# A two-block transformer step on one core: first expert choice by single heads, zero products on TensorE, other places for early weights, state stores on SyncE

## The reference

```python
q = (xb @ w_q).reshape(P_TOKEN_BLOCK, P_HEADS, 2, P_DKEY // 2)
s = jnp.einsum('tphd,phnd->tphn', q, subkeys)
s1, i1 = lax.top_k(s[:, :, 0], P_TOPK)
s2, i2 = lax.top_k(s[:, :, 1], P_TOPK)
cand = (s1[..., :, None] + s2[..., None, :]).reshape(...)
cidx = (i1[..., :, None] * P_NKEYS + i2[..., None, :]).reshape(...)
top, pos = lax.top_k(cand, P_TOPK)
eidx = jnp.take_along_axis(cidx, pos, axis=-1)
g = jax.nn.softmax(top, axis=-1)
act = jax.nn.gelu(jnp.einsum('tped,td->tpe', u[eidx], xb))
return jnp.einsum('tpe,tped->td', g * act, v[eidx])
```

## Time and profile before

| | us |
|---|---|
| three timed runs | 2357.81, 2358.45, 2362.10 |
| median | 2358.45 |
| profiled execution | 2352.93 |
| its span, first to last instruction | 2351.0 |

### The profile page before, as it was taken

The page is one execution under the profiler, slowest core; times in us unless marked ns, Lnnn a source line. Parts: engine busy times, 40 slices in busy tenths (PEclk is TensorE's granted clock), DMA queues, the critical chain, the costliest instruction groups (busy, mean ns, idle before and its releaser), DMA issues. The chain is left out here.

```text
span 2351.0 us, 28978 instructions
## 1 busy us (share of the span) xinstructions
PE 1575.8 (67%) x9366; PEld 844.4 (36%) x9366; DVE 1567.6 (67%) x4325; ACT 841.5 (36%) x2753; POOL 858.4 (37%) x772
## 2 busy tenths in 40 slices
PE   8888976885855446656756677797766445555555
PEld 6775633653521112324522344455433102100010
DVE  2357987556768876565697567864865897665654
ACT  2324354533323223443233435533322334232232
POOL 0013343333325343333335333343544444444351
PEclk8998988998877778877878798888888777777776
DMA  9979999999999999999999999999999999999996
GB/s 388 408 262 415 380 400 405 422 421 401 412 421 421 421 422 421 421 422 405 420 419 372 418 421 421 419 421 415 395 420 422 417 422 421 421 421 421 422 422 276
DMA packets 145003, 956.47 MB, mean 407 GB/s; under 512 B 17749, under 2 KB 20437, under 8 KB 35797
## 3 DMA queue, kind: packets, MB, share of 16 engines
q0 software_dynamic: 110592, 805.36, 82.7%
q1 hardware_dynamic: 28928, 145.20, 15.3%
q10 hardware_dynamic: 5332, 4.07, 0.8%
HBM read 951.67 MB, written 2.89 MB: 406 GB/s over the span
## 5 line engine op out<-in xcount | busy, mean ns | idle before, releaser
L825 POOL DMA_INDIRECT rows<-in_uv,eidx x768 | 858.2, 1117 | 1453.7 <-PE acc L913 1075.0
L1488 DVE CUSTOM_DVE_ANT_0 rows<-rows,xrep 128x1024 f32<-128x1024 f32 x768 | 913.2, 1223 | 403.6 <-DMA rows<-in_uv,eidx 370.1
L913 PE MATMUL acc<-rows,diag 128*32 128x512 f32 x3072 | 754.5, 742 | 513.2 <-ACT diag L1167 477.6
L913 PEld LDWEIGHTS acc<-rows,diag 128*32 128x32 f32 x3072 | 154.7, 126 | 1008.6 <-ACT diag L1167 634.3
L1167 ACT ACTIVATE act_out<-act_in 128x2 f32<-128x2 f32 x384 | 77.7, 202 | 978.8 <-DVE act_in L1488 930.6
L843 PE MATMUL bank<-wt,hT 128*128 128x256 f32 x888 | 207.4, 394 | 22.2 <-DMA wt<-in_attn_w_qkv 6.9
L1167 ACT ACT_TABLE_LOAD x120 | 154.0, 1283 | 167.0 <-DVE act_in L1488 86.7
L1167 ACT ACTIVATE diag<-small,wv 128x32 f32<-128x32 f32 x768 | 204.8, 314 | 12.5
L843 PEld LDWEIGHTS bank<-wt,hT 128*128 128x128 f32 x888 | 174.0, 198 | 63.2 <-issue 25.8
L843 PE MATMUL bank<-hT,wt 128*128 128x256 f32 (+1 forms) x896 | 182.6, 369 | 15.7 <-ACT hT L1167 8.2
L1167 ACT ACTIVATE wv<-act_out,gate 128x1 f32<-128x1 f32 x768 | 184.3, 287 | 12.6
(11 more groups left out here) (186 smaller groups left out, 1375.8 us busy)
## 6 DMA issues: line engine op xcount, KB each, us to landing
wt<-in_ada_w SPq DMA_DIRECT2D x24, 1024.0 KB
wt<-in_peer_w_q SPq DMA_DIRECT2D x24, 1024.0 KB
rows<-in_ada_w SPq DMA_DIRECT2D x36, 512.0 KB, 15.0
wt<-in_mlstm_w_in SPq DMA_DIRECT2D x12, 1024.0 KB
rows<-in_uv,eidx POOLq DMA_INDIRECT x768
wt<-in_attn_w_qkv SPq DMA_DIRECT2D x12, 1024.0 KB
rows<-in_mlstm_w_in SPq DMA_DIRECT2D x21, 512.0 KB, 15.9
rows<-in_peer_w_q SPq DMA_DIRECT2D x16, 512.0 KB, 13.9
```

Of the source, the lines that this page charges most:

```text
L825: nc.gpsimd.indirect_dma_start(out=rows[:, r, :], out_offset=None, in_=A["uv"], in_offset=bass.IndirectOffsetOnAxis(ap=eidx[:, b, slot:slo ...
L913: last = nc.tensor.matmul(acc[c:c + QUAD, h * 512:(h + 1) * 512], diag[:, r, :], rows[:, r, D + h * 512:D + (h + 1) * 512], start=first, s ...
L1488: last = V.tensor_tensor_reduce(out=rows[:, r, 0:D], in0=rows[:, r, 0:D], in1=xrep[:, GS * odd + j, :], scale=1.0, scalar=0.0, op0=ALU.mul ...
```

## The change

Five edits, all in the stretch from the start to the end of the first phase of groups:

- **One head at a time.** `PQ` and `PS` of the first quarter are split by head. `PT`, `PC` and `PG` of head 0 follow on VectorE as soon as head 0's scores are there; its scores and pair sums use memory of `eidx` and `gate` instead of the arena. The state update (`MLU`) and the modulation part `MR 1 0` move from ahead of or behind the choice to between the two heads, `XR` behind it. Slots are dealt to quadrants four ways (16 moves of 4 columns instead of 8 of 8), and the first two gathers are released after half of the moves, the next after all.
- **Zero products** (`FILLERS`) at seven places of the first 140 us.
- **Other places.** `LAP` starts the early places at place 9, so that the first round ends with places 0 to 8, and `last_early` becomes the step of query quarter 2 and its keys; the loads behind it are late tiles.
- **State stores** are issued by SyncE, behind the last early load; the wait for them moves from `PC` of the first head to the copy of the scores of quarter 2.
- **Sample statistics.** The norm's squares and roots of the two sample blocks (`STAT`) are computed behind the prompt's head norm; both blocks are then normalised into separate memory (`normed`) early in the groups. `DEALS` and `PATIENCE` of the phase (0, 0) have new numbers.

```diff
-    (0, 0): [0, 0, 0, 1, 0, 0, 0, 0, 1, 0, 0, 0, 1, 2, 0, 0, 0, 2, 0, 0, 0, 0, 5, 0, 1, 0, 0, 3, 0, 0, 1, 0, 1, 0, 1, 0, 3, 2, 1, 0, 0, 1, 0, 1, 2, 1, 0, 0, 1, 1, 1, 2, 0, 0, 0, 0, 0, 2, 4, 0, 0, 2, 0, 2, 0, 1, 0, 1, 0, 0, 5, 0, 1, 0, 1, 1, 0, 0, 0, 0, 6, 0, 0, 0, 0, 0, 1, 0, 0, 2],
+    (0, 0): [1, 0, 1, 1, 0, 1, 0, 2, 0, 1, 0, 2, 0, 0, 0, 2, 0, 0, 0, 0, 1, 1, 0, 0, 2, 0, 3, 2, 0, 3, 0, 0, 1, 0, 1, 1, 1, 2, 0, 1, 3, 1, 0, 0, 0, 0, 0, 0, 2, 0, 2, 0, 1, 0, 4, 0, 1, 1, 1, 0, 1, 4, 0, 0, 1, 0, 0, 2, 0, 2, 0, 4, 0, 1, 1, 0, 0, 0, 0, 0, 2],
...
-    yield from (*mod(0, 2), ("MLN", "P", 0), ("MLO", "P", 2), ("MLO", "P", 3), ("MLM", "P", 0), *mod(0, 3), ("T2", 0, "P"))
+    yield from (*mod(0, 2), ("MLN", "P", 0), ("STAT",), ("MLO", "P", 2), ("MLO", "P", 3), ("MLM", "P", 0), *mod(0, 3), ("T2", 0, "P"))
...
-    yield from (("NT", 0, 1, 0), *cell(["MLU"], 0), *cell(["MLU"], 1), ("STATE",))
-    yield from (("PQ", 0, "P", 0), ("PS", 0, "P", 0, 0), ("PQ", 0, "P", 1), ("XR", 0, 0, 0), ("XR", 0, 0, 1))
-    yield from ((k, 0, "P", 0, 0, half) for half in range(2) for k in ("PT", "PC", "PG"))
-    yield from (("PW", 0, "P", 0, 0, half) for half in range(2))
-    rest = [("PS", 0, "P", 0, 1), ("PQ", 0, "P", 2), ("PS", 0, "P", 0, 2), ("PQ", 0, "P", 3), *mod(1, 0)]
+    yield ("NT", 0, 1, 0)
+    for head in range(2):
+        yield from (("PQ", 0, "P", 0, head), ("PS", 0, "P", 0, 0, head))
+    yield from (("PQ", 0, "P", 1), ("PT", 0, "P", 0, 0, 0), ("PC", 0, "P", 0, 0, 0), ("PG", 0, "P", 0, 0, 0))
+    yield from (*cell(["MLU"], 0), *cell(["MLU"], 1), *mod(1, 0))
+    yield from (("PT", 0, "P", 0, 0, 1), ("PC", 0, "P", 0, 0, 1), ("PG", 0, "P", 0, 0, 1), ("PS", 0, "P", 0, 1))
+    yield from (("XR", 0, 0, 0), ("XR", 0, 0, 1), ("PW", 0, "P", 0, 0))
...
-    start = [*quarter[1], ("PS", 0, "P", 0, 3), *later[0:6], *quarter[2], *later[6:9], *quarter[3]]
+    start = [*norms, ("PQ", 0, "P", 2), quarter[1][0], ("PS", 0, "P", 0, 2), ("PQ", 0, "P", 3), quarter[1][1], *turned, quarter[1][2],
+             ("PS", 0, "P", 0, 3), *later[4:6], *quarter[2], *later[6:9], *quarter[3]]
...
+LAP = [*range(WRING + 4, EARLY), *range(WRING + 4)]
...
-    last_early = PLAN.index(("MR", 1, 0, 3))
+    last_early = PLAN.index(("PS", 0, "P", 0, 2))
...
-                    load(src[:, c:min(c + HALF * WC, n)], len(loads) % EARLY, last)
+                    load(src[:, c:min(c + HALF * WC, n)], LAP[len(loads) % EARLY], last)
...
+FILLERS = {("NT", 0, 0, 0): 3, ("MLD", "P", 0, 0): 1, ("MLW", "P", 1, 0): 5, ("MLA", "P", 0, 0): 1, ("T2", 0, "P"): 2, ("MR", 0, 4, 1): 2, ("NT", 0, 1, 0): 3}
...
+                if n == EARLY_LOADS:
+                    for d in range(2):
+                        last = of(("MLU", "P", d, 0)) + MH - 1
+                        sp.wait_ge(by(last), emptied(last))
+                        sp.dma_start(O["new_C"][0, 0, d].rearrange("h p v -> p h v"), cell("P", d)[2][:, :, 0:DV]).then_inc(state_out, 16)
+                        sp.dma_start(O["new_n"][0, 0, d].rearrange("h p -> p h"), cell("P", d)[2][:, :, DV], allow_slow_non_contiguous=True).then_inc(state_out, 16)
+                        sp.dma_start(O["new_m"][0, 0, d:d + 1, :], mst[0:1, d, :]).then_inc(state_out, 16)
...
-                    if g % QG == 0 or g == QG // 2:
-                        pool.wait_ge(experts_chosen, g // QG + 1 + (g > 0))
+                    if g % QG == 0 or g in (1, QG // 2):
+                        pool.wait_ge(experts_chosen, g // QG + 1 + (g > 0) + (g > 1))
...
+                if PLAN[n_entry - 1] in FILLERS:
+                    for _ in range(FILLERS[PLAN[n_entry - 1]]):
+                        fill(WC)
...
+                    for a in range(2):
+                        e = 2 * s[5] + a
+                        last = mm(t[:, a * NKEYS:(a + 1) * NKEYS], qTp[:, e, 0:P], first_keys[:, e * NKEYS:(e + 1) * NKEYS], True, True)
...
+                elif k == "STAT":
+                    act.wait_ge(sample_in, 16)
+                    rsqrt_parts([x[:, b, :] for b in BLOCKS["S"]], Nflat[:, 0:D], KEPT)
...
-                elif k == "STATE":
-                    for d in range(2):
-                        last = of(("MLU", "P", d, 0)) + MH - 1
-                        act.wait_ge(by(last), emptied(last))
-                        act.dma_start(O["new_C"][0, 0, d].rearrange("h p v -> p h v"), cell("P", d)[2][:, :, 0:DV]).then_inc(state_out, 16)
...
+                    if s == ("PS", 0, "P", 0, 2):
+                        dve.wait_ge(state_out, 96)
...
-                    if s[1:] == (*FIRST_SCORES[1:], 0):
-                        dve.wait_ge(state_out, 96)
...
+                        for q in range(QUADS):
+                            for kk in range(QUADS):
+                                last = V.scalar_tensor_tensor(experts[quadrant(kk), q], chosen[0][quadrant(q), kk], 1.0 / PACK,
+                                                              chosen[1][quadrant(q), kk], ALU.mult, ALU.add)
+                            if q == QUADS - 1 or (q == 1 and half == [0]):
+                                last.then_inc(experts_chosen, 1)
```

156 lines of the change are left out of this document (98 added, 58 removed).

## The result

| | median us | runs | ratio to the kernel before |
|---|---|---|---|
| before | 2357.26 | 7 | |
| changed | 2369.17 | 7 | 1.0057 [1.0042, 1.0071] |

What follows compares the result with a forecast made beforehand. The prediction took DMA, bytes over rate plus time with idle queues, to bound the kernel. Its terms, -8.7 + 13.3 + 2.0 - 8.0 = -1.4 us, put on the median 2358.45 gave 2357.0 us, range 2347 to 2366.

Steps and rivals of the forecast that it cites:

- Term 1: From the start to the first gather: a shorter chain and zero products issue it earlier, -8.7 us, between -7.0 and -10.7.
- Term 2: Behind the first gather: the stream must now carry 5.5 MB of late weights and state stores, +13.3 us.
- Term 3: State stores beside gathers: 4-byte normaliser elements take more than their bytes are worth, +2.0 us, bounds 0.6 and 6.1.
- rival (c): State stores beside gathers: elements go one at a time and cost 6.1 us, total +2.7, 2361 us; chance 8%.
- Term 4: First phase of groups: earlier sums close the holes at 235, 300 and 400 us, -8.0 us, between 0 and -11.5.
- rival (a): GpSimd's wait for group 7's sum: if later than about 226 us, bytes not given back, +5.6, 2364 us; chance 18%.

Runs made afterwards that it cites:

- experiment 6: Kernel before with all 1024 normaliser elements of 4 bytes stored behind its last weights, then half there and half in the tail: 1.0031 and 1.0012.
- Experiments 1, 2 and 4: Changed kernel without the normaliser stores (0.9969), with them stored behind the last gather (0.9978), with them turned into 32 runs of 128 bytes (0.9973).
- experiment 4: Changed kernel with normalisers turned on VectorE and stored at the same place of SyncE's queue in 32 runs of 128 bytes: 2349.89 us, 0.9973.

## Why the prediction was wrong

**Term 1, the first gather: right in its parts, too small in size.** 8.7 us were expected (7.0 to 10.7), 11.3 were seen. The shorter chain from hT to the numbers came as worked out: 150.09 - 133.90 = 16.2 us from the first query product to the gather, against 161.43 - 138.11 = 23.3. The queries started at 133.90, not at 136.7 (137.5 less the 0.8 expected ahead of the chain). The zero products had been given 1.7 us ahead of the chain and a price of 1.3 in it; they gave 7 (158.1 against 150.8, one execution each), since they also kept the gates' products and the queries at 2.4 GHz, and their price there could not be measured.

**Term 2, the bytes: right, by a count and not by a run of its own.** -11.3 + 13.3 asks for a lag of 2.0 us; 2.7 were counted at 164 us.

**Term 3, the stores beside gathers: this step failed.** It said +2.0, between 0.6 and 6.1. The runs with the tail store and with the turned one put it at 18.6 and 19.8 us. Two errors are in it. The first is the size of the rate. It was taken from the share of the 256-byte packets in the earlier trace rows, which beside gathers cost no rate at all; the choice of that row over the one with the very same store was wrong, and even the other row counts only the elements' own time, while the gather packets beside them grew from 0.28 to 0.50 us: 7 to 8 us by experiment 6 and by the run with ScalarE's queue (which has TensorE's wait of 9.5 us in it). The second is that the term had only a rate and no path through compute. The modulation that now stands between the heads met the stores: ScalarE stood until 163.06, TensorE lost its clock, the sum of group 0 and the issue of quarter 3's weights came 12.5 us late, the weights took 7 us longer, and the sum of group 7 came at 249.6 instead of 230.2, which empties the ring again between 260 and 330 us. The other 11 us are read from these rows; no run separates them further. Experiments 1, 2 and 4 show that the elements at this place cause ScalarE's stop, for none of the three has it, nor has the run with the elements in ScalarE's own queue. How they do is open: the profile only calls the releaser remote. The wait of VectorE, costed at nothing, was 3.39 us. The prediction listed what was queued behind that moved wait, but not what else the moved stores would make late.

The Trainium skill (DMA: Bandwidth & Descriptors, Rules for kernel authors) tells to rearrange so that the last dimension is contiguous, since otherwise each element gets a descriptor; the rule was cited as rival (c) and given 8%. The trace agrees with the rule (129 packets with 0.00 MB between them), and experiment 4 does what it says.

**Term 4, what compute gives back: right in kind, and undone by term 3.** Its size, 8.0 us, was not measured by itself. With the stores in the tail the shares at the places of the earlier trace rows are 1.02. The sum of group 7 comes at 230, not at 211 as I had added up, and that was enough. In the changed kernel it came at 249.6. So rival (a) had the right place. Its turning point of 226 us was too early, since a sum at 230.2 left no hole. Its cause, row spreading and quarter 3's weights behind the first gather, is harmless without the elements, and with the rate loss outside of it it had half of the size.

**The sum with what was measured.** -11.3 + 13.3 + 0 - 8.0 = -6.0 us without the element stores beside the gathers; the two runs with the tail store and the turned one gave 0.9978 and 0.9973, -5.2 and -6.4. So terms 1, 2 and 4 hold together, each by itself less surely. With 18.6 to 19.8 for term 3 the sum is +12.6 to +13.8 and 13.4 were measured; that adds nothing new, since term 3 is itself the difference to these two runs.

## A version that beats both

The kernel before with the zero products and the tail store: 2347.84 us, 0.9967 [0.995, 0.9983]. The changed kernel with the elements in the tail and eleven zero products is as good (2348.41 us, 0.997). So the head-by-head choice, the later weights and the new deals show no gain of their own: they start the stream some 6 us earlier (150.8 against 156.35) and close the hole at 235 us (share 1.02 against 0.58), and carry 5.5 MB more behind the start, which is 13.3 us.

## What to carry to other kernels

A store that is moved out of a hole of the DMA into a full stream is to be priced by a row of the same store, not by its bytes and not by a row of larger packets; what its landing and its issue can make late, on every engine, is to be listed as for a wait. If its last dimension is strided, turn it on an engine first or leave it for the tail. Of a chain that starts a bandwidth-bound stream, the pauses of TensorE ahead of long products are worth filling: here the kernel before with zero products and the tail store is as fast as the best form of the change. And a run that adds a wait along with a cost needs a twin with the wait alone.
